# First attention of a two-block transformer: the products for the modulation begin one step later

## The reference, cut to what matters

```python
for l in range(DEPTH):                                  # DEPTH = 2
    mod_lat = silu_c @ w_ada[l] + b_ada[l]              # 1024 -> 3072: shift, scale, gate
    mod_ctx = silu_cc @ w_ada[l] + b_ada[l]
    x, ctx = _layer(x, ctx, mod_lat, mod_ctx, ...)
# in _layer
xn = _rms_norm(x, g_norm) * (1 + sc[:, None]) + sh[:, None]
... = _split_proj(xn @ w_in)                            # a gated MLP, attention, a recurrence
s = einsum('bqkgd,bskd->bkgqs', q, k) * ATTN_SCALE
o = einsum('bkgqs,bskd->bqkgd', softmax(s), v)
x = x + gt[:, None] * (concatenate([y_a, y_b, y_c]) @ w_out)
```

## Time and profile before

| | |
|---|---|
| Median of 3 runs | 1080.14 us (1079.84 to 1081.03) |
| The profiled execution: its own time | 1079.62 us |
| Its span in the profile | 1077.8 us |
| Mean granted TensorE clock | 0.999 |
| PE busy | 1067.4 us, 99% of the span |
| DVE, ACT, POOL busy | 717.8, 572.5, 141.2 us |
| Moved by transfers | 168.77 MB, mean 157 GB/s |
| First attention, from its first scores to the end of its last weighing | about 193.3 to 268.8 us |

### The profile page before, as it was taken

One profiled execution on the slowest core, in us unless ns is written; L12 is line 12 of the kernel. 1 busy time (PEld: TensorE's weight loads), 2 busy tenths in 40 slices (PEclk: granted clock), 3 DMA queues, 4 the chain that ended last, 5 costly groups with the idle time before them and its releaser, 6 DMA issues.

```text
span 1077.8 us, 19907 instructions
## 1 busy us (share of the span) xinstructions
PE 1067.4 (99%) x8092; PEld 949.7 (88%) x8092; DVE 717.8 (67%) x1224; ACT 572.5 (53%) x971; POOL 141.2 (13%) x166
## 2 busy tenths in 40 slices
PE   9999999999999999999999999999999999999998
PEld 6887878656898998799899999999997799999997
DVE  5665566386554868778865676666677776766674
ACT  4532675544444466866565554444574555444454
POOL 0000010253200001632531000000023410000000
PEclk9999999999999999999999999999999999999999
DMA  9742121387513432056454364555543334555551
GB/s 383 316 142 69 66 78 40 110 282 243 189 40 119 150 134 79 4 194 234 147 167 157 118 235 161 192 189 168 198 151 113 123 118 157 196 195 176 213 179 39
DMA packets 25386, 168.77 MB, mean 157 GB/s; under 512 B 3280, under 2 KB 3536, under 8 KB 5456
## 3 DMA queue, kind: packets, MB, share of 16 engines
q1 hardware_dynamic: 25152, 167.25, 43.9%
q10 hardware_dynamic: 144, 0.26, 0.1%
HBM read 164.35 MB, written 1.05 MB: 153 GB/s over the span
## 4 chain that ended last, share of the span: by engine, by line
PE 90%; DVE 3%; ACT 2%; DMA 2%; POOL 1%; issue 1%; SPq 0%; DVEq 0%; ACTq 0%
PE bank L437 25%; PE bank L438 24%; PE bank L439 24%; PE bank L1655 2%; DMA PROJ<-in_stream 2%; PE bank L1520 2%; PE bank L1675 2%; PE bank L494 2%; PE bank L1665 1%; DVE wlo L415 1%; PE bank L1547 1%; PE bank L2318 1%; POOL TILE L1616 1%; ACT TILE L1709 1%; PE bank L1538 1%
## 5 line engine op out<-in xcount | busy, mean ns | idle before, releaser
L437 PE MATMUL bank<-OPH,whi 128*128 128x256 f32 (+1 forms) x1716 | 519.8, 303 | 1.0 <-DVE wlo L415 0.7
L439 PE MATMUL bank<-OPH,wlo 128*128 128x256 f32 (+1 forms) x1716 | 511.2, 298 | 0.0
L438 PE MATMUL bank<-OPL,whi 128*128 128x256 f32 (+1 forms) x1716 | 511.2, 298 | 0.0
L415 DVE TENSOR_TENSOR wlo<-raw,whi 128x1024 fp32r<-128x1024 f32 (+1 forms) x255 | 304.5, 1236 | 103.0 <-ACT whi L400 103.0
L437 PEld LDWEIGHTS bank<-OPH,whi 128*128 128x128 f32 x1716 | 328.0, 191 | 18.6 <-issue 5.6
L438 PEld LDWEIGHTS bank<-OPL,whi 128*128 128x128 f32 x1716 | 328.2, 191 | 10.0 <-issue 1.2
L439 PEld LDWEIGHTS bank<-OPH,wlo 128*128 128x128 f32 x1716 | 328.0, 191 | 9.8
L400 ACT ACTIVATE whi<-raw 128x1024 fp32r<-128x1024 f32 (+1 forms) x255 | 254.8, 1050 | 75.1 <-PE bank L439 72.8
L437 PE MATMUL bank<-whi,OPH 128*128 128x256 f32 (+2 forms) x272 | 93.8, 345 | 0.0
L438 PE MATMUL bank<-wlo,OPH 128*128 128x256 f32 (+2 forms) x272 | 91.1, 335 | 0.0
L439 PE MATMUL bank<-whi,OPL 128*128 128x256 f32 (+2 forms) x272 | 91.1, 335 | 0.0
(11 more groups left out here) (281 smaller groups left out, 1124.1 us busy)
## 6 DMA issues: line engine op xcount, KB each, us to landing
raw<-in_stream SPq DMA_DIRECT2D x143, 1024.0 KB, 4.9
PROJ<-in_stream SPq DMA_DIRECT2D x5, 1024.0 KB, 18.4
raw<-in_stream SPq DMA_DIRECT2D x4, 1056.0 KB, 8.5
PROJ<-PROJ SPq DMA_DIRECT2D x32, 64.0 KB, 3.9
FIRST<-in_first SPq DMA_DIRECT2D x1, 1248.0 KB, 5.9
C<-in_con SPq DMA_DIRECT2D x1, 1157.5 KB, 7.4
FIRST<-in_first SPq DMA_DIRECT2D x1, 1024.0 KB, 7.9
WST<-in_w_s SPq DMA_DIRECT2D x2, 256.0 KB, 7.3
```

The source lines that it names most:

```text
L415: nc.vector.tensor_tensor(c.w[1][:, part], c.raw[:, part], c.w[0][:, part].bitcast(F32), ALU.subtract).then_inc(*raises(c.lo[h]))
L437: nc.tensor.matmul(out, w[0], x[0], start=start, stop=False, skip_group_check=skip)
L438: nc.tensor.matmul(out, w[0], x[1], start=False, stop=False, skip_group_check=skip)
L439: return nc.tensor.matmul(out, w[1], x[0], start=False, stop=stop, skip_group_check=skip)
```

## The change

```
@@ AdaBeside.step
-                if n == self.steps - 2:
+                if n == self.steps - 3:
                     split(e, self.after.s + 0.5)
@@ the loop over the steps of the attention
                 if j in between:
                     between[j]()
-                if l == 0 and j < mod.steps:
-                    attend_step(f"attn{l}_chunk", "chunk", mod, j)
+                if l == 0 and 0 < j <= mod.steps:
+                    attend_step(f"attn{l}_chunk", "chunk", mod, j - 1)
                 if l == 0 and j in (at.n, at.n + 1):
                     open_output((0,) if j == at.n else (1, 2, 3))
```

## The result

| | before | after |
|---|---|---|
| Median of 12 runs each | 1079.89 us (1079.68 to 1081.03) | 1082.22 us (1080.63 to 1083.94) |
| Ratio | | 1.0018, 95% interval 1.0011 to 1.0026 |
| Span of the profiled execution | 1077.8 us | 1080.4 us |
| Mean granted clock of it | 0.999 | 0.998 |

The ratio makes +1.9 us (1.2 to 2.8), the medians +2.3, the profiled execution +2.6. Forecast was +1.6 and 1081.7; the measured time lies in the range, but a part of it has another cause than the sum had.

A forecast was written before the change was run, and what follows sets the result against it. PE, busy 99% of the span, was taken as the bound. Opening later (264.3 - 263.1) plus the last turn (0.44) gave +1.6 us, 1081.7 us against the median 1080.14; range 1079.6 to 1083.2.

The forecast's parts named there:

- the sum: Whole kernel: opening later, 264.3 - 263.1, plus the last turn's 0.44, makes +1.6 us.
- part 4: First output-weight load: issued later, lands at 260.32 after 5.2; ACT waits some 1.9 us, `wlo` starts at 261.73 (261.82 before).
- part 5: Bank 0 at the output opening: DVE's copy of pair 7's rows queues behind `wlo`; opening 264.3, not 263.10; PE idles some 2.9.
- The earlier gain: Steps before the opening: moving the turn ends waits at steps 5, 9, 13, at most 1.11 us; unit 15's scores at 255.65.
- part 2: Not all gained: about 0.2 of step 5's 0.37 returns as a wait in step 6; unit 1's turn waits 0.36 more.
- the wait that comes back behind unit 5: Step 6: DVE and ACT's exponentials run behind, so about 0.2 of the 0.37 gained at step 5 is lost.
- my two bounds: Extra wait for POOL at unit 1: 0.4 with POOL at 2.56 us, 0 at about 2.0; 0.36 taken.
- a rival's chance: Behind the opening: PE's clock falls in the 2.9 us idle, costing 1.5 us, total +3.1; chance 0.08.
- the last turn: Pair 7's turn now lies between the opening and the last weighing, adding 0.44 us.
- the launch's pace: Fallen-clock price: 4 us behind the idle at 7 passes per microsecond in place of 11, costing 1.5 us.
- the lower end of the range: Whole kernel: 1079.6 us, if the bank is not late, less the runs' spread of about 0.5.
- Part 6: Behind the opening: PE bound by its own products, second `wlo` half causes no wait, every later stage moves as a whole.

The follow-up runs named there:

- experiment 1: Changed kernel with output jobs of banks 0 and 1 exchanged and the last pair's turned rows in bank 0: 1080.37 us, ratio 1.0004 to the kernel before.
- experiment 2: Changed kernel with the first output-weight chunk loaded one place earlier, ahead of the last modulation chunk: 1079.58 us, ratio 0.9993 to the kernel before.
- experiment 3: Changed kernel with both the bank exchange and the earlier load of the first output weights: 1078.98 us, ratio 0.9992 to the kernel before.
- the execution at 0.995: Profiled run of the changed kernel measured again (experiment 7), mean granted clock 0.995: 1085.51 us.
- experiment 6: Changed kernel with the earlier load and banks exchanged only for the first four output jobs: 1078.72 us, ratio 0.9985 to the kernel before.
- experiment 8: Kernel before, with only DVE's copy of the last pair's rows put behind its lower half of the weights: 1080.69 us, ratio 1.0004.
- experiment 7: Changed kernel measured once more, unaltered, for the spread: 1082.24 us (1080.84 to 1085.51), ratio 1.0016 to the kernel before.

## Why the prediction was right, and where it was not

**The place and both terms of the wait were right.** Parts 4 and 5 gave a late load and a copy queued behind `wlo`. Experiments 1 and 2 take away one each, experiment 3 both: PE's idle ahead of the opening goes from 2.65 to 1.49, 0.88 and none, and the opening from 263.76 to 262.36, 261.93 and 261.06 (in experiment 1 product 15 itself starts 0.25 sooner, at 259.80). The chain from product 13 to the opening was forecast at 264.3 - 255.06 = 9.2 us and took 263.76 - (253.75 + 1.07) = 8.9. The landing was 4.9, not 5.2. So `wlo` started 0.53 sooner than before, where part 4 had all of the gain used up.

**The earlier gain was sized nearly right, by errors that offset each other.** Unit 15's scores were forecast at 255.65 and came at 255.34. The wait of 0.36 at unit 1 (part 2) did not come, and the pause that stood in that turn before (1.26 for it in the earlier trace rows, 1.09 after) went too: the scores of unit 4 came 1.09 sooner, and the sum had 1.00 - 0.36 = 0.64. With the product moved as well, POOL started unit 1 at 209.45, 1.64 behind scores 2, as forecast, but took 2.04 and not the 2.56 of the earlier trace rows; I had taken the wrong one of my two bounds. Against that, the wait that comes back behind unit 5 was 0.52, not 0.2, so that the first round of four units gained nothing (the sum had 0.17): it is met by the scores of unit 7, which wait for the exponentials of unit 6, and those for DVE. The two later rounds gained 0.39 each, as forecast (0.37).

Why POOL took 2.04 this time can be read from the rows of DVE beside it, the first row before, the others after:

```profile
211.48 0.68 DVE L1082 TENSOR_TENSOR OPL<-PROJ,OPH 128x512 fp32r<-128x512 f32 x1
```

```profile
209.45 2.04 POOL L1730 TENSOR_TENSOR TILE<-TILE,STAT 128x512 f32<-128x512 f32 x2 [4.74 <-DVE STAT L1721]
211.28 0.76 DVE L1082 TENSOR_TENSOR OPL<-PROJ,OPH 128x512 fp32r<-128x512 f32 x1
...
220.90 2.04 POOL L1730 TENSOR_TENSOR TILE<-TILE,STAT 128x512 f32<-128x512 f32 x2 [2.49 <-DVE STAT L1721]
222.09 1.40 DVE L1082 TENSOR_TENSOR OPL<-PROJ,OPH 128x512 fp32r<-128x512 f32 x1
```

Before, DVE's instruction lay in the middle of POOL's two, and POOL's took 0.5 longer; after, it began 0.2 ahead of POOL's end. At 222.09 the same instruction lay beside POOL again, and this time DVE's took twice its 0.68. So where both are at work one of them takes longer, and it is not always the same one; why, no run separates.

**The step that failed is a rival's chance.** Opening 0.66 late, the last turn 0.4: that is +1.1 us, and the runs at full clock lie near it (1080.63 to 1080.94 against a median of 1079.89). The rest, 7.60 - 6.01 = 1.6 us in the profiled execution, is the fallen clock. I gave that 0.08; by the mean clocks it came in 8 of 12 runs and in 7 of 11. Its price, +1.5 from the launch's pace, is near the 1.6 measured, but that too is two errors that offset: I took 7/11 of the pace over 4 us, and it was half the pace over 3.4. In the execution at 0.995 it was 2.9. That the longest idle in this stretch was 0.69 only meant that no row of the stretch told; it is no evidence against a fall. And the trace of the kernel before does have a row on it that I passed over, at its end, behind PE's last matmul:

```profile
1072.30 0.39 PE L439 MATMUL bank<-whi,OPL 128*128 128x512 f32 x1
```

```profile
1076.00:1077.00 1.00, 0.00 (x0) 0.00 (x0) 0.00 (x0) 0.00 (x0) 0.00 (x0) 0.66 0.88 318
1077.00:1078.00 1.00, 0.00 (x0) 0.00 (x0) 0.00 (x0) 0.00 (x0) 0.00 (x0) 0.50 0.00 0
```

There PE had been idle for 3.6 us when the clock fell. That is longer than the 2.9 forecast, so it settles nothing, but it shows the clock falling behind an idle of this very kernel, and speaks for more than 0.08. At the same place in the profile of the execution at 0.995 the fall comes 2.0 us behind the last matmul.

So the forecast of +1.6 is near the measured +1.9 in part by luck: a wait forecast 0.5 too late stands where part of the clock's cost should be. One sum does not come out, without weight: the lower end of the range, 1079.6, by its own terms (1080.14 + 0.4 - 0.5) is 1080.0.

The Trainium skill (TensorE: Matmul & The Clock Gate, "What's actually happening") says that the clock has two levels and is halved after the engine has idled, and this was the rule against the change. The traces agree: 0.5 behind 2.65 us of idle in both profiles of the changed kernel, 1.00 behind 1.49, 1.37 and 0.88. For the slow pace at a kernel's start the same section has a spread from run to run of one kernel; here, in the middle of a kernel, the half level lasted 3.4 us in one execution and 6.8 in another.

The estimate by the Trainium skill (DMA: Bandwidth & Descriptors, "Anatomy of one DMA"), 4.4 us for 1 MB, was too low by 0.5 against 4.9 here. The section gives its fit for transfers issued by GpSimd; these are issued by SP, so it is not a test of the fit.

**Part 6 held.** Every later stage moved as a whole: the end of the weighings moved by 271.36 - 268.72 = 2.64, the span by 2.6. The same reckoning holds in experiment 2 (-0.8 in the span). In experiments 1 and 3 it breaks by 0.6, through the exchange of banks itself. In experiments 6 and 8 the profiled spans are 0.3 and 0.4 longer than the reckoning gives, which is less than spans of one kernel differ by.

**Still open.** Why some executions of the same kernel kept the full clock and others did not, and why the return took 3.4 or 6.8 us, was not tried. Nor was the idle length between 1.49 and 2.65 at which it begins to happen. The runs of experiments 1, 2, 3, 6, 7 and 8, and of the kernel before, that lie some 1 us over the rest at the same mean clock have their extra time outside the span, before the first or after the last instruction (but for one run of experiment 1, whose span itself is 1079.3); what takes it there is not shown.

## What to carry to other kernels

When a step of background work is moved, follow the buffers that it leaves behind and not only its instructions: here the last product's bank was the next stage's first one, and the copy that frees it stood behind a split that waited for a load that was itself released one step later. Price a long idle of TensorE twice, once for itself and once for the matmuls behind it at half clock: here 2.65 us of idle cost another 1.6 or 2.9 us in 15 of 23 executions, and 1.49 us cost nothing more. If it can't be removed, matmuls without use may pay for themselves. When the runs of a kernel spread more than before, compare their mean granted clocks and their spans first: runs that differ in both point to such an idle, runs that differ only in what lies outside the span do not.

## What was not expected of the hardware

- With the same program the granted clock fell in 15 of 23 runs, by their mean clocks and spans. In the two profiled ones the idle was 2.65 us both times, the half level lasted 3.4 us and 6.8, and the cost was 1.6 and 2.9 us. In one of them the clock fell while PE idled, in the other when it was back at work.
- 1.49 us of idle left the clock at 1.00 in the profiled execution of experiment 1, and no run of it shows a mean under 0.999.
- 3.15 us of unneeded matmuls in an idle of 2.65 us took 1.1 us off the median (1081.16 against 1082.24, measured on two occasions, each beside a kernel before at 1080.3 to 1080.4).
